# Two forgetting heads at a time, gates added by TensorE, and softmax division moved behind the value product

## The reference, cut to what matters

```python
h = hybrid_mixer(x)              # branches A, B, C in parallel, then an output projection
x = layer_norm(ALPHA * x + h)
x = layer_norm(ALPHA * x + memory_cross_attention(x, mem))
x = layer_norm(ALPHA * x + swiglu(x))
# branch B: windowed attention, 8 query heads on 2 key heads, learned sinks
p = exp(s - m); denom = sum(p) + exp(sink - m); o = (p / denom) @ v
# branch C: forgetting attention, 4 heads of width 64
c = cumsum(log_sigmoid(fgate_logit))            # per position and head
s = q_i @ k.T + c_i[:, None] - c_k[None, :]     # where kpos <= qpos, else -1e30
o = softmax(s) @ v
```

## Time and profile before

| | us |
|---|---|
| median of 3 runs | 922.24 |
| lowest and highest | 921.06, 927.32 |
| the profiled execution's own time | 923.17 |
| its span, first to last instruction | 921.4 |
| self-attention stage in it (first transpose of probabilities to first gate piece) | 195.46 to 270.78 |

### The profile page before, as it was taken

How to read it: one execution, slowest core, us unless ns; L and a number is a source line. 1 busy time by engine, 2 the same in 40 slices (tenths; PEclk the granted TensorE clock), 3 DMA queues, 4 the chain that set the end, 5 groups by cost and what they waited for, 6 DMA issues and landing times.

```text
span 921.4 us, 11604 instructions
## 1 busy us (share of the span) xinstructions
PE 890.2 (97%) x4511; PEld 734.9 (80%) x4511; DVE 438.4 (48%) x833; ACT 297.9 (32%) x552; POOL 69.8 (8%) x103
## 2 busy tenths in 40 slices
PE   7999999988989999999999889999999999999996
PEld 7988897776558888888889769888888888888885
DVE  3344356589662625252766775344333333322344
ACT  3112166137753222322323653222222222211221
POOL 2100000162420000000011010000000000000001
PEclk9999999999899999999999899999999999999998
DMA  7525522320002322225522211222223324222321
GB/s 264 156 91 137 115 92 57 105 92 2 1 1 80 103 92 92 91 91 213 197 93 87 98 47 46 92 91 91 91 96 111 112 91 137 91 92 92 100 107 68
DMA packets 70023, 89.89 MB, mean 98 GB/s; under 512 B 2701, under 2 KB 61911, under 8 KB 69983
## 3 DMA queue, kind: packets, MB, share of 16 engines
q1 hardware_dynamic: 69599, 88.92, 29.7%
q0 software_dynamic: 384, 0.43, 0.3%
HBM read 86.81 MB, written 2.52 MB: 97 GB/s over the span
## 4 chain that ended last, share of the span: by engine, by line
PE 87%; DVE 5%; ACT 4%; issue 1%; DMA 1%; POOL 1%; DVEq 0%; SPq 0%; POOLq 0%; ACTq 0%
PE ps L1578 26%; PE ps L1579 26%; PE ps L1580 26%; ACT prob L825 2%; PE ps L1763 2%; PE ps L1737 1%; PE ps L1712 1%; PE ps L1615 1%; DVE prob L1189 1%; DVE w_lo L1066 1%; DVE prob L1168 1%; DMA x_nat<-in_x 1%; PE ps L2036 1%; PE ps L2037 1%; PE ps L2038 1%
## 5 line engine op out<-in xcount | busy, mean ns | idle before, releaser
L1578 PE MATMUL ps<-xt_hi,w_hi 128*128 128x512 f32 (+1 forms) x712 | 274.6, 386 | 4.5 <-DVE xt_lo L1072 2.1
L1580 PE MATMUL ps<-xt_lo,w_hi 128*128 128x512 f32 (+1 forms) x712 | 273.7, 384 | 0.0
L1579 PE MATMUL ps<-xt_hi,w_lo 128*128 128x512 f32 (+1 forms) x712 | 273.7, 384 | 0.0
L1578 PEld LDWEIGHTS ps<-xt_hi,w_hi 128*128 128x128 f32 x712 | 133.8, 188 | 32.8 <-DVE w_lo L1066 2.4
L1580 PEld LDWEIGHTS ps<-xt_lo,w_hi 128*128 128x128 f32 x712 | 133.8, 188 | 26.5
L1579 PEld LDWEIGHTS ps<-xt_hi,w_lo 128*128 128x128 f32 x712 | 133.8, 188 | 26.4
L803 ACT CAST w_hi<-raw 128x1024 fp32r<-128x1024 f32 (+1 forms) x59 | 60.9, 1035 | 184.2 <-PE ps L1580 172.7
L1066 DVE TENSOR_TENSOR w_lo<-raw,w_hi 128x1024 fp32r<-128x1024 f32 (+1 forms) x59 | 71.2, 1210 | 96.9 <-ACT w_hi L803 96.6
L1534 DVE TENSOR_TENSOR w_lo<-raw,w_hi 128x1024 fp32r<-128x1024 f32 x40 | 48.9, 1222 | 79.1 <-ACT w_hi L1025 79.1
L1355 DVE TENSOR_TENSOR w_lo<-raw,w_hi 128x1024 fp32r<-128x1024 f32 x30 | 36.7, 1223 | 91.5 <-ACT w_hi L951 91.5
L1025 ACT CAST w_hi<-raw 128x1024 fp32r<-128x1024 f32 x40 | 41.9, 1047 | 78.8 <-PE ps L1580 78.8
(11 more groups left out here) (246 smaller groups left out, 1315.6 us busy)
## 6 DMA issues: line engine op xcount, KB each, us to landing
raw<-in_w_in SPq DMA_DIRECT2D x24, 1024.0 KB, 5.0
raw<-in_w_ffn_in SPq DMA_DIRECT2D x22, 1024.0 KB, 4.9
raw<-in_w_ffn_out SPq DMA_DIRECT2D x11, 1024.0 KB, 4.8
raw<-in_w_mix_out SPq DMA_DIRECT2D x4, 1024.0 KB, 4.9
x_nat<-in_x SPq DMA_DIRECT2D x4, 512.0 KB, 6.5
raw<-in_w_branch_b SPq DMA_DIRECT2D x4, 512.0 KB, 3.9
resid<-in_x SPq DMA_DIRECT2D x1, 2048.0 KB, 9.6
raw<-in_w_xkv SPq DMA_DIRECT2D x2, 1024.0 KB, 5.9
```

The source lines that it names most:

```text
L1578: pe.matmul(dst, a_hi, b_hi, start=start, stop=False)
L1579: pe.matmul(dst, a_lo, b_hi, start=False, stop=False)
L1580: return pe.matmul(dst, a_hi, b_lo, start=False, stop=stop)
```

## The change

Four edits belong together.
1. Branch C in row-half pairs: keys of two heads share a tile (two tiles, no zeros; one drain for a piece of keys), and scores of an even and an odd head are computed in turn on the two row halves of TensorE, in banks next to each other. Job 8 holds three of the four query tiles of heads 0 and 1, job 9 the fourth of both, jobs 10 and 11 the same for heads 2 and 3, and they are computed in iterations 10, 11, 12, 14, 15 and 16.
2. Gates on TensorE: `cum` is split into three BF16 parts, turned by eight BF16 matmuls into `gates_t` (two copies, for the two row halves), and added onto the scores in PSUM by a BF16 matmul with `pick`, a constant of minus ones and zeros that selects a head's three rows. The query's own gate is left out, since the softmax cancels it. The causal mask becomes the bias table of line 1168. The base rows of ScalarE and the masking by GpSimd are gone.
3. Branches B and C are divided at the drain: probabilities stay unscaled; GpSimd spreads the reciprocals of a pair of heads over 64 columns each (`widen`), TensorE turns them by four transposes (`turn_recip`) into the bank that the next pair will use, ScalarE copies them to SBUF (`recip_copy`), and VectorE multiplies the accumulators by them while draining (`out_drain`).
4. The two heads of a pair (in A: the two parts of one head) share one accumulator bank, one in each half of the partitions, and banks 6 and 7 alternate by pair. Jobs 1 and 3 alone are scaled by GpSimd.

```diff
+C_SCORES_AT = [10, 12, 14, 16]
...
-        at = [2048 * h + a for a in C_AT]
-        banks = [[("C", h, 0, 0, 128, at[0]), ("C", h, 2, 128, 384, at[2])],
-                 [("C", h, 1, 0, 256, at[1])], [("C", h, 3, 0, 512, at[3])]]
+        pair, at = h - h % 2, [2048 * h + a for a in C_AT]
+        heads = [(i, [2048 * i + a for a in C_AT]) for i in (pair, pair + 1)]
+        if h == pair:
+            banks = [[("C", i, 0, 0, 128, a[0]), ("C", i, 2, 128, 384, a[2])] for i, a in heads]
+            banks += [[("C", i, 1, 0, 256, a[1])] for i, a in heads]
+        else:
+            banks = [[("C", i, 3, 0, 512, a[3])] for i, a in heads]
+        units = [("C", h, t, 0, (t + 1) * P, at[t]) for t in range(TT)]
...
-        items = ([("base", j, 0)] if j >= 8 else []) + [("bank", j, b) for b in range(len(jobs[j][0]))]
-        for i, item in enumerate(items):
-            side[2 * j - 7 + i // 2].append(item)
+        first = 2 * j - 7 if j < 8 else C_SCORES_AT[j - 8]
+        for b in range(len(jobs[j][0])):
+            side[first + b // 2].append((j, b))
...
+    def acc_bank(m):
+        return 6 + (m if m >= FIRST_X else m // 2) % 2
...
+            def widen(k):
+                kind, h, _ = acc_kind[2 * k]
+                c = stat_col(kind, h, 0)
+                pool.wait_ge(rsum_ready, k - N_AH + 1)
+                if k - 2 >= N_AH:
+                    pool.wait_ge(recip_ps, k - 2 - N_AH + 1)
+                pool.tensor_copy(qk[:, T_WIDE + k % 2, :].rearrange("p (t h d) -> p t h d", t=TT, h=2),
+                                 rsum[:, c:c + 2 * TT].rearrange("p (h t) -> p t h", t=TT).unsqueeze(3).to_broadcast([P, TT, 2, DH])
+                                 ).then_inc(recip_wide, 1)
+            pool.wait_ge(neg_ready, units_before[N_AH])
+            widen(N_AH)
+            widen(N_AH + 1)
+            pool.wait_ge(av_done, groups_before[N_AH])
+            pool.wait_ge(neg_ready, units_before[8])
+            pool.wait_ge(acc_dve, N_AH)
+            for m in range(N_OUT_AB):
+                if m >= 2:
+                    pool.wait_ge(acc_dve, m + 3)
+                if m >= 1:
+                    widen(N_AH + m + 1)
...
+            def recip_copy(k):
+                act.wait_ge(recip_ps, k - N_AH + 1)
+                act.wait_ge(acc_dve, k - 1)
+                act.copy(qk[:, T_RECIP + k % 2, :], ps[:, acc_bank(2 * k + 2), :]).then_inc(recip_out, 1)
...
+            for i in range(N_GROUP_PAIRS):
                 if i + 1 < N_GROUP_PAIRS:
                     pt_drain(2 * i + 2)
+                if i - 1 in out_end[:N_AH]:
+                    first_part(out_end.index(i - 1))
                 if i == 0:
                     split(PG + 1)
+                if i in RECIP_AT:
+                    recip_copy(N_AH + RECIP_AT.index(i))
+                for j, b in SIDE[i - 1] if i else []:
+                    exps(j, b)
...
+            def out_drain(k):
+                kind, h, _ = acc_kind[2 * k]
+                bank = acc_bank(2 * k)
+                dve.wait_ge(av_done, acc_end[2 * k + 1] + 1)
+                if kind == "A0":
...
+                else:
+                    dve.wait_ge(recip_out, k - N_AH + 1)
                     tile = {"B": T_QB, "C": T_QC}[kind] + h // 2
+                    dve.tensor_tensor(qk[:, tile, :], ps[:, bank, :], qk[:, T_RECIP + k % 2, :], ALU.mult).then_inc(acc_dve, 1)
...
+                    link(dve.tensor_tensor(cum[:, :, :], cum[:, :, :], cum3[:, :, 2, :], ALU.add))
+                    left = fl[:, 0, :, :]
+                    link(dve.tensor_copy(cparts[:, :, :, 0], cum[:, :, :]))
+                    link(dve.tensor_tensor(left, cum[:, :, :], cparts[:, :, :, 0], ALU.subtract))
+                    link(dve.tensor_copy(cparts[:, :, :, 1], left))
+                    link(dve.tensor_tensor(left, left, cparts[:, :, :, 1], ALU.subtract))
+                    dve.tensor_copy(cparts[:, :, :, 2], left).then_inc(cum_ready, 1)
...
-                    dve.tensor_scalar(ncum_t[:, :], ps[0:N_CH, 3, :], -1.0, None, ALU.mult).then_inc(cumt_out, 1)
+                    dve.wait_ge(const_ready, 6)
+                    for at in (0, 64):
+                        dve.tensor_copy(gates_t[at:at + 3 * N_CH, :], ps[at:at + 3 * N_CH, 3, :]).then_inc(cumt_out, 1)
...
+                for j in range(N_AH, N_SELF):
+                    if SUMS_AT.get(j) == i:
                         sums_out(j)
+                if i - 1 in out_end:
+                    out_drain(out_end.index(i - 1))
+                for jj, b in SIDE[i]:
+                    scores_out(jj, [b])
+            out_drain(N_OUT - 1)
...
+                return qk[half_, T_QC + h // 2, rows], qk[half_, T_KC + h // 2, 0:(t + 1) * P]
+            def key_gates(h, n):
+                half_ = slice(64 * (h % 2), 64 * (h % 2) + 64)
+                return pick[half_, h % 2, h // 2:h // 2 + 1].to_broadcast([64, P]), gates_t[half_, 0:n]
...
-                            ins = pe.matmul(ps[:, score_bank(j, b), c0:c0 + cols], q, k, start=True, stop=True)
-                            if u == n_units - 1:
+                            ins = pe.matmul(ps[:, score_bank(j, b), c0:c0 + cols], q, k, start=True, stop=kind != "C")
+                            if u == n_units - 1 and kind != "C":
                                 ins.then_inc(score_ps, 1)
+                        for b in some:
+                            kind, h, t, c0, cols, at = JOBS[j][0][b][u]
+                            if kind == "C":
+                                one, gates = key_gates(h, cols)
+                                ins = pe.matmul(ps[:, score_bank(j, b), c0:c0 + cols], one, gates, start=False, stop=True)
+                                if u == n_units - 1:
+                                    ins.then_inc(score_ps, 1)
...
-                pe.wait_ge(prob_pool if j in POOL_SCALES else prob_dve, scaled_for(j, g))
+                if N_AH <= j < N_SELF:
+                    pe.wait_ge(exp_done, exps_of(j))
+                else:
+                    pe.wait_ge(prob_pool if j in POOL_SCALES else prob_dve, scaled_for(j, g))
...
+            def turn_recip(k):
+                pe.wait_ge(recip_wide, k - N_AH + 1)
+                pe.wait_ge(acc_dve, k)
+                for t in range(TT):
+                    cols = slice(t * P, (t + 1) * P)
+                    ins = pe.transpose(ps[:, acc_bank(2 * k + 2), cols], qk[:, T_WIDE + k % 2, cols], ident[:, :])
+                ins.then_inc(recip_ps, 1)
...
-                    if first and m >= 2:
-                        if acc_kind[m - 2][0] == "X":
-                            pe.wait_ge(oxl_done, m - 2 - (N_ACC - N_XACC) + 1)
-                        else:
-                            pe.wait_ge(acc_dve if acc_by_dve[m - 2] else acc_act, acc_count[m - 2])
+                    if first and m >= FIRST_X + 2:
+                        pe.wait_ge(oxl_done, m - 2 - FIRST_X + 1)
+                    elif first and 4 <= m < FIRST_X:
+                        pe.wait_ge(acc_dve, m // 2 - 1)
+                        if m // 2 > N_AH:
+                            pe.wait_ge(recip_out, m // 2 - N_AH)
...
-                    for t in range(TT):
-                        ins = pe.transpose(ps[0:N_CH, 3, t * P:(t + 1) * P], cum[:, t, :], ident[:, :])
+                    for at in (0, 64):
+                        for t in range(TT):
+                            ins = pe.matmul(ps[at:at + 3 * N_CH, 3, t * P:(t + 1) * P],
+                                            cparts[:, t, :, :].rearrange("p h c -> p (h c)"), shift[:, 384:384 + P], start=True,
+                                            stop=True)
...
+                if SIDE[i]:
+                    scores(SIDE[i][0][0], [b for _, b in SIDE[i]])
+                if i in RECIP_AT:
+                    turn_recip(N_AH + RECIP_AT.index(i))
```

More of the change, by code:

```diff
@@ L197, in make_jobs @@
                   ([at[2] + 2 * P, at[3] + 2 * P], [(2, 0, 256, 256)], "C", h, False, True)]
[L198 removed]
+        jobs.append((banks, groups, units))
     return jobs
@@ L1321, in _ @@
             pt_drain(1)
-            for i in range(N_GROUP_PAIRS + 1):
-                for m in accs_ended[2 * i - 2] if i else []:
-                    acc_drain(m)
-                if i == N_GROUP_PAIRS:
-                    break
+            for i in range(N_GROUP_PAIRS):
                 if i + 1 < N_GROUP_PAIRS:
```

222 lines of the change are left out of this document (73 added, 149 removed).

## The result

| | before | after |
|---|---|---|
| median of the runs beside each other, us | 924.46 (6 runs) | 908.91 (6 runs) |
| lowest and highest | 921.06, 928.23 | 908.46, 909.77 |
| ratio after / before | | 0.9836, 95% interval 0.9817 to 0.9856 |
| span of the profiled execution | 921.4 | 907.8 |
| self-attention stage in it, start and end | 195.46, 270.78 | 197.59, 257.75 |

The forecast was 910.0 us (906 to 917), faster. In the two profiles the span fell by 13.6 us. The stage gives 15.16 of it; 2.13 are given back ahead of it (it starts that much later), and 0.6 is saved behind it.

A forecast was written before the change was run, and what follows sets the result against it. TensorE was taken to bound nearly everywhere, waiting on VectorE in branch A, with VectorE itself the bound in branch C. Terms -7.3 + 3.0 - 6.5 - 3.3 + 1.05 = -13.05 us from 923.17 gave 910.1, rounded to 910.0 (906 to 917).

The forecast's parts named there:

- Scores and gates: Forgetting heads on TensorE: row-half pairs and BF16 gates cut 14.0 us to 6.7, a gain of 7.3 us.
- The rival that pairs don't pay: Forgetting heads' scores and gates stay at 14.0 us, giving 917.3 us; chance 0.05.
- Turned reciprocals: Branches B and C: 24 added transposes of reciprocals on TensorE, all on the path, cost 3.0 us.
- Waits: Self-attention stage: of TensorE's 8.87 us idle, 6.5 us go and 2.4 stay.
- the microsecond for seams: Self-attention stage: one microsecond of TensorE idle time kept for seams the layout does not show.
- the exponentials' 1 us: End of the stage: TensorE waits about 1 us for the last two heads' exponentials, replacing the 2.7 us scaling wait.
- The pace in branch A: Branch A iterations: TensorE's own work becomes the bound at 3.0 us each, with VectorE at 2.7.
- ScalarE's rival: ScalarE sets the pace: 14 iterations take 3.35 instead of 3.0 us, giving 914.9 us; chance 0.14.
- The clock: Between branches A and C: the 6.60 us at half clock return to full clock, saving 3.3 us.
- The rival that the half clock returns there: Self-attention stage: the half clock comes back, so 3.3 us are not won, giving 913.3 us; chance 0.12.
- Ahead of the stage: Before the stage: five linked VectorE instructions cutting cumulative gates delay low weights TensorE waits for, costing 1.05 us.
- The slower chain for the reciprocals: Branches B and C: GpSimd split, broadcast, turn and copy make each of six pairs late, giving 927.5 us; chance 0.04.

The follow-up runs named there:

- the run head by head: Kernel after, with forgetting heads' scores in jobs 8 and 10 issued one head after the other, so one row half follows itself: 912.67 us.
- the run with the parts cut later: Kernel after, with the five instructions cutting the cumulative gates into parts moved behind the low weights that TensorE waits for: 907.32 us, ratio 0.9825.
- shared banks alone: Kernel before, with only the accumulator banks changed so that the two heads of a pair share one: 921.26 us, ratio 0.9983.
- Without division: Kernel before, with the division by row sums in branches B and C left out and banks unchanged: 915.88 us, ratio 0.9901.
- without division and with shared banks: Kernel before, with the division of branches B and C left out and pairs of heads sharing a bank: 913.11 us, ratio 0.9867.
- the added multiplications: Kernel after, with 40 VectorE multiplications on a scratch tile added in iterations 4, 5 and 8 to 15: 911.08 us, ratio 0.9852.

## Why the prediction was right

Its sum was 910.1 us and the profiled execution took 909.56; 910.0 was forecast and 908.91 is the median. The ratio's interval is clear of no change by the 1% that a measurement of this kernel can tell. That the sum is met to half a microsecond is partly luck: the stage fell by 1.1 us more than its four terms say (15.2 against 14.1), and the slower pace of the first 15 us, of which the sum has no term, took 1.0 back. Two small slips stand in the text: its own terms make the stage 61.2 us long, not "some 62", and the chances it adds to 0.72 come to 0.71. By its own steps:

- **Scores and gates, -7.3 us**: 6.7 us were forecast to be left, and 3.35 + 3.36 were. From start to start two heads' scores take 2.53 us of it (2.49 forecast) and their gates 0.82 (0.85). That pairs overlap is shown by the run head by head. The rival that pairs don't pay is out. The Trainium skill's rule on weight loads (TensorE: Matmul & The Clock Gate, "Weight-path perf modes"), which the prediction weighed, agrees with the row here: 95 ns a load against 182 for FP32, also with a column step of zero. No row shows what the loads would have cost the path otherwise.
- **Turned reciprocals, +3.0 us**: six turns take 0.53 to 0.59 us from start to start, 3.3 in all. Turning twice adds 2.6, so 0.11 for each transpose; the six turns hold 24 x 0.11 = 2.6 us and some 0.1 each for the start of a burst, which my 0.128 a transpose, from one burst of eight, did not carry. This term was 0.3 too small.
- **Waits, -6.5 us**: TensorE's idle time fell from 8.87 to 1.53 us (60.16 less 58.63), so 7.3 went. The 2.4 that I let stand were too many: of the microsecond for seams nothing came, while the exponentials' 1 us and the start's 0.3 were there. The reason given was right, and more so than I thought for a time: bank and VectorE's load are two limits, and the prediction had both, the bank as a wait and the load in the pace of branch A.
- **The pace in branch A**: 3.0 us an iteration were forecast from TensorE's own work. Products at 203.03 and 223.82 are seven iterations apart, 2.97 us each. VectorE was busy for 20.05 of these 20.79 us, 2.9 an iteration and not the 2.7 forecast, so its margin was 0.1 us and not 0.2 to 0.3. ScalarE's rival (3.35) did not come true; it was busy for 18.25 of them.
- **The clock, -3.3 us**: 1.00 throughout the stage. What the half clock had cost can be read from the same five bursts of two heads in the kernel before: 8.23 us for the first (229.85 to 238.08) and 5.02 for the second (240.12 to 245.14), so 3.2 us. The rival that the half clock returns there did not come true in any of the nine profiles of this form.
- **Ahead of the stage, +1.05 us**: 1.09, and the run with the parts cut later gives 1.06 back.
- **The slower chain for the reciprocals**: TensorE waited for none of the six pairs. GpSimd's broadcast took 0.61 us, half of the 1.27 I had taken from its subtraction, and the sums were ready in time.

The stage's parts add to -7.3 + 3.3 - 7.3 - 3.2 = -14.5 us of the 15.16 measured. Of the 0.7 left, 0.2 is that eight transposes ahead of a turn take 0.93 us (224.84 to 225.77) instead of 1.02, twice; the rest I did not place.

The time came out 1.1 us below the forecast in the median, and the idle time of the stage was 0.9 us less than forecast. This is not a proof of each term to a tenth: the same kernel's median moved by 1.3 us between two sets of runs (908.91 and 910.23).

## What to carry to other kernels

Two limits that end in one wait are priced separately: taking away the wait that the profile names (the bank, 3.4 us) moved the stage by 2.1 us and the time by 1.2, since VectorE's full queue stood right behind it, and taking away the load left the bank. Compare such runs over the same work, here seven iterations, and not over the same times. A group's mean can hide two kinds: look at its shortest and longest before a cost is read from it. Matmuls that contract over 64 rows gained here only where the other row half was next in the queue; look at the order in which units are issued, not at their shapes. And five instructions of 0.2 us cost 1.1 us for no other reason than their place in a queue, ahead of something that TensorE was already waiting for.

## What the runs showed of the hardware that was not expected

**The half clock in the stage** fell at the same work, the gates of the first forgetting head, in both profiles of the kernel before and with shared banks alone, each time right behind four microseconds in which TensorE was busy for about half the time or less (2.27, 2.18 and 1.73 us); here the second run of the kernel before:
```profile
225.00:229.00 4.00, 2.18 (x16) 1.43 (x16) 3.87 (x15) 2.19 (x9) 1.65 (x2) 1.00 0.00 0
229.00:230.00 1.00, 0.83 (x1) 0.38 (x2) 1.00 (x5) 0.00 (x0) 0.00 (x0) 0.66 0.00 0
230.00:231.00 1.00, 1.00 (x2) 0.00 (x0) 0.76 (x3) 0.00 (x0) 0.00 (x0) 0.50 0.00 0
```
The gap alone does not decide it. Without division the four microseconds ahead of the gates were busy for 3.10 us, and the clock stayed; without division and with shared banks they were busy for 3.04, and it fell all the same, 2.1 us behind the start of the gates and for 3.4 us (1.6 us lost); and the four microseconds of the earlier trace rows with 1.33 us busy were followed by none. In the kernel after, the four microseconds around its longest wait (248 to 252 us) hold 2.92 us of TensorE. That it stays away in all nine profiles of that form is shown; what exactly triggers it is not.

**The clock outside the stage differs between runs of one kernel.** Between 505 and 535 us the same kernel was granted the full clock in one profile and 0.72 over ten microseconds in another (the kernel before: its first profile 0.94 and 0.72 from 515 to 535 us, its second 1.00 and 1.00), and the stage of the kernel after began at 197.59 us in one and at 196.94 us in the other profile, with one and the same front; that of the kernel before at 195.46 and 194.80. In these four profiles, in the same order, the record of the granted clock begins at 14.0, 12.8, 11.8 and 10.9 us, and the matmuls of the first weight piece ahead of it are 0.21 us apart instead of 0.12 (the last has none ahead of it). A difference of 1 to 2 us between two profiles of this kernel is therefore read from the stage's own length, which repeats to 0.03 us, and not from the span.

**A multiplication of VectorE can stand behind a subtraction of GpSimd.** Four of the added multiplications took 1.29 to 1.33 us instead of 0.27, each for as long as a subtraction of GpSimd (1.27 to 1.32 us) ran beside it. The kernel before shows the same with its own scalings: those of the last forgetting head but one took 2.77 us while GpSimd split an output tile, those of the last, in the same four sizes, 1.27 with GpSimd idle.
```profile
259.33 2.77 DVE L1189 TENSOR_SCALAR prob<-prob,rsum 128x128 f32<-128x128 f32 x4
260.29 1.27 POOL L779 TENSOR_TENSOR o_lo<-qk,o_hi 128x512 fp32r<-128x512 f32 x1
264.15 1.27 DVE L1189 TENSOR_SCALAR prob<-prob,rsum 128x128 f32<-128x128 f32 x4
```
VectorE's reading of the last scores stood in its queue behind these 2.77 us, and on that reading hung the 2.7 us wait of the earlier trace rows. How much of the wait came from it was not tried.
